# Six row slots instead of eight in a two-layer pooling, attention and expert kernel, with the memory used to keep weight pieces

## What is computed

```python
q = (h @ w_q).reshape(B, S, 8, 2, 128)
s = einsum('bshpc,hpnc->bshpn', q, sub_keys)        # 128 keys in each half
top_s, top_i = top_k(s, 16)                         # then 16 of the 16x16 sums
...
a = einsum('tkd,td->tk', u[ii], hh)                 # 8 heads x 16 experts for each token
w = gg * gelu(a)
return einsum('tk,tkd->td', w, v[ii])
...
x = x + sigmoid(rmsnorm(x) @ ple_wg) * (p @ ple_wp)
```

## Time and profile before

| | |
|---|---|
| Median of 3 runs | 2981.84 us (2978.21 to 2984.22) |
| The profiled execution: time, span | 2986.85 us, 2985.0 us |
| TensorE, VectorE, ScalarE, GpSimd busy | 77%, 74%, 36%, 43% |
| Row gathers, share of the DMA engines | 87.6% |
| Weights and constants, share of the DMA engines | 8.2% |
| Moved in all | 1178.01 MB, mean 395 GB/s |
| Granted TensorE clock, mean | 0.898 |

### The profile page before, as it was taken

The page is one execution under the profiler, slowest core; times in us unless marked ns, Lnnn a source line. Parts: engine busy times, 40 slices in busy tenths (PEclk is TensorE's granted clock), DMA queues, the critical chain, the costliest instruction groups (busy, mean ns, idle before and its releaser), DMA issues.

```text
span 2985.0 us, 23741 instructions
## 1 busy us (share of the span) xinstructions
PE 2284.8 (77%) x6832; PEld 1225.6 (41%) x6832; DVE 2214.6 (74%) x4418; ACT 1074.5 (36%) x3178; POOL 1284.5 (43%) x1028
## 2 busy tenths in 40 slices
PE   3687667977779897888777989789876888665555
PEld 3453224532435454454343545445533444231113
DVE  4585967896687867766979877676596797877774
ACT  1343333333333433643233343355322244333222
POOL 0343453445434444544333444454333344455551
PEclk7889898989989999999988999899998899887777
DMA  4999999999999999999989999999997999999993
GB/s 175 411 364 422 401 420 421 377 420 420 420 380 404 408 421 421 420 420 421 416 331 392 408 408 421 421 408 395 422 420 317 420 381 416 420 419 421 420 420 166
DMA packets 164931, 1178.01 MB, mean 395 GB/s; under 512 B 18496, under 2 KB 19904, under 8 KB 23488
## 3 DMA queue, kind: packets, MB, share of 16 engines
q0 software_dynamic: 147456, 1073.81, 87.6%
q1 hardware_dynamic: 16768, 100.59, 8.2%
q10 hardware_dynamic: 576, 2.10, 0.2%
HBM read 1174.32 MB, written 2.10 MB: 394 GB/s over the span
## 4 chain that ended last, share of the span: by engine, by line
DMA 36%; PE 28%; DVE 24%; issue 5%; ACT 5%; POOL 2%; SPq 0%; ACTq 0%; DVEq 0%; POOLq 0%
DMA slot<-in_uv,idx 35%; PE acc L832 16%; DVE slot L1416 8%; PE M L553 3%; DVE X L1409 3%; PE B L553 2%; POOL slot L530 2%; PE B L625 2%; PE M L625 1%; ACT diag L1028 1%; DVE pos_u L1110 1%; DVE SC L1105 1%; ACT w L1022 1%; DVE best L1108 1%; DVE pos_u L1106 1%
## 5 line engine op out<-in xcount | busy, mean ns | idle before, releaser
L832 PE MATMUL acc<-slot,diag 128*128 128x512 f32 x2908 | 1562.4, 677 | 646.8 <-ACT diag L1028 643.6
L530 POOL DMA_INDIRECT slot<-in_uv,idx x1024 | 1284.3, 1254 | 1644.6 <-PE acc L832 1107.0
L1416 DVE CUSTOM_DVE_ANT_0 slot<-slot,HP 128x1024 f32<-128x1024 f32 x1024 | 1244.9, 1221 | 612.4 <-DMA slot<-in_uv,idx 590.0
L832 PEld LDWEIGHTS acc<-slot,diag 128*128 128x128 f32 x2908 | 574.4, 210 | 1475.9 <-ACT diag L1028 897.7
L1020 ACT ACTIVATE act_a<-a 128x1 f32<-128x1 f32 x1024 | 207.0, 202 | 1705.2 <-DVE a L1416 1692.9
L1409 DVE SCALAR_TENSOR_TENSOR X<-slot,w,X 128x1024 f32<-128x1024 f32 x297 | 380.6, 1281 | 16.5 <-ACT w L1022 16.4
L1022 ACT ACTIVATE w<-act_a,gate 128x1 f32<-128x1 f32 x1024 | 301.6, 295 | 33.2
L1028 ACT ACTIVATE diag<-cst,w 128x128 f32<-128x128 f32 x727 | 291.9, 402 | 23.8
L553 PE MATMUL B<-w,TT 128*128 128x256 f32 x400 | 90.7, 379 | 0.0
L553 PE MATMUL M<-w,TT 128*128 128x256 f32 x400 | 90.6, 379 | 0.0
L625 PE MATMUL M<-TT,w 128*128 128x256 f32 (+1 forms) x448 | 89.7, 356 | 0.0
(11 more groups left out here) (169 smaller groups left out, 1568.1 us busy)
## 6 DMA issues: line engine op xcount, KB each, us to landing
w<-in_wq SPq DMA_DIRECT2D x28, 1024.0 KB
slot<-in_uv,idx POOLq DMA_INDIRECT x1024
w<-in_ple_wg SPq DMA_DIRECT2D x8, 1024.0 KB
w<-in_w_o SPq DMA_DIRECT2D x8, 1024.0 KB
w<-in_w_dq SPq DMA_DIRECT2D x6, 1024.0 KB
w<-in_w_uq_nope SPq DMA_DIRECT2D x8, 768.0 KB
w<-in_ple_wp SPq DMA_DIRECT2D x5, 1024.0 KB
slot<-in_wq SPq DMA_DIRECT2D x4, 1024.0 KB, 10.3
```

Source lines behind the costliest of these rows:

```text
L530: nc.gpsimd.indirect_dma_start(out=slot[s][:], out_offset=None, in_=uv[g // NC], in_offset=bass.IndirectOffsetOnAxis(ap=idx[:, g % HPB, k: ...
L832: last = nc.tensor.matmul(acc[:, half * 512:half * 512 + 512], diag[adds_on_pe(n) % DIAGS][:], slot[s][:, D + half * 512:D + half * 512 + ...
L1416: nc.vector.tensor_tensor_reduce(out=slot[s][:, 0:D], in0=slot[s][:, 0:D], in1=HP[:, g % HPB, :], scale=1.0, scalar=0.0, op0=ALU.mult, op1 ...
```

## The change

SLOTS goes from 8 to 6. A row slot has the size of one weight piece (2048 floats for each of 128 partitions, 1 MB), and the memory of the two slots becomes two places "more" of one piece each, MORE = 2. Pieces 4 and 5 of wq (layer 0) are loaded into them for pair 1 and used again for the group of pairs 2 and 3. After that the two key-value weights w_ukv_k and w_ukv_v are loaded into them for group 4 and used again for group 6. The first of those loads waits for the last use of the wq piece that lay there. Since 128 is no multiple of 6, slots are numbered n % SLOTS over all gathers.

```diff
-SLOTS = 8
+SLOTS = 6
+MORE = 2
...
 KEPT = [("wq", (1, 2)), ("ple_wg", (4, 6, 7))]
+MORE_KEPT = [(("wq", 4), (1, 2)), (("wq", 5), (1, 2)), (("w_ukv_k", 0), (4, 6)), (("w_ukv_v", 0), (4, 6))]
...
+        more = [(j, groups) for j, (kept_piece, groups) in enumerate(MORE_KEPT)
+                if (name, i) == kept_piece and g0 in groups]
         if n < FIRST_PIECES:
             found.append(("slot", FIRST_SLOT + n, 0, None, False))
         elif kept:
             k, groups = kept[0]
             found.append(("KV", i, k, None, g0 != groups[0]))
+        elif more:
+            j, groups = more[0]
+            home = "more", j % MORE
+            if g0 == groups[0] and home in first:
+                had = first[home]
+            else:
+                had = None
+            first[home] = n
+            found.append(home + (j // MORE, had, g0 != groups[0]))
...
+        more = [sb(f"more{i}", [P, PIECE]) for i in range(MORE)]
...
+                    "more": [sem(f"more_loaded{i}") for i in range(MORE)],
...
-                if where == "ring" and had is not None:
+                if where in ("ring", "more") and had is not None:
                     sp.wait_ge(weights_used, had + 1)
...
-                    n, s = g * KSEL + k, k % SLOTS
+                    n, s = g * KSEL + k, (g * KSEL + k) % SLOTS
...
-                s = k % SLOTS
+                s = n % SLOTS
```

More of the change, by code:

```diff
@@ L377, in trunk @@
         slot = [sb(f"slot{i}", [P, 2 * D]) for i in range(SLOTS)]
-        places = {"ring": ring, "slot": slot, "KV": [KV[:, i * PIECE:(i + 1) * PIECE] for i in range(4)]}
+        more = [sb(f"more{i}", [P, PIECE]) for i in range(MORE)]
+        places = {"ring": ring, "slot": slot, "more": more, "KV": [KV[:, i * PIECE:(i + 1) * PIECE] for i in range(4)]}
         diag = [sb(f"diag{i}", [P, P]) for i in range(DIAGS)]
@@ L1015, in gather @@
                 g, k = divmod(n, KSEL)
-                s, half = k % SLOTS, k // (KSEL // 2)
+                s, half = n % SLOTS, k // (KSEL // 2)
                 if k % (KSEL // 2) == 0:
@@ L1405, in add_late @@
                     g, k = divmod(n, KSEL)
-                    s, Xc = k % SLOTS, X[:, g % NC, :]
+                    s, Xc = n % SLOTS, X[:, g % NC, :]
                     dve.wait_ge(weighted, n + 1)
```

## The result

The changed kernel takes 3052.86 us in the median (3052.63 to 3055.03, 4 runs), the kernel before 2980.3 (2978.21 to 2984.22, 4 runs). The ratio is 1.0239, 95% interval 1.0224 to 1.0253: 72.6 us slower. The forecast was +56, with +15 to +105 by its bounds; the way is right, and three terms of the sum turned out to be wrong in size, in both directions.

The account below looks back on a forecast made before the run. The prediction took DMA transfers, mostly row gathers, to bound the kernel, with slots mattering where the consumer is late. Full bursts +50, partial stretches +16 and bytes -10 gave +56 us on 2981.8: 3038 us, range 2997 to 3100.

Parts of the forecast that it names:

- The bound and the cover: Row gathers: DMA-bound; a slot's turn needs 11.8 us, leaving 8.2 us against a late consumer with eight slots, 3.2 with six.
- rival C: Every gather, ordinary stretches too: stage work holds slots longer than 15.0 us, 87 us on top, 3125 us; chance 0.15.
- Rival A: Every stretch: the cover is enough and only bytes count, -10 us, so 2972 us; chance 0.07.
- Rival B: Bursts cost a gather at four or five places only, about +10, cancelled by -10: no change, 2982 us; chance 0.06.
- The bytes, -10: Weight queue: four 1024 KB loads less, 2.49 us each where the DMA is full; -10.0 us, bounds 5 to 10 saved.
- The ten full bursts, 5.0 us each: Ten stretches where eight slots ran out: each pays two gathers once, 5.0 us; +50 in all, bounds +25 to +55.
- The partial stretches, +16: Nine dense stretches at 420 to 422 GB/s where eight slots just held: 1.8 us each, +16, bounds 0 to +45.
- My +0: DMA idle at 1505 and 2246, GpSimd waiting for VectorE's indices: doesn't hang on slots, +0, up to +10.

Follow-up runs that it names:

- the put-in bursts: Unread sums put on VectorE in the last pair, five bursts of 6 us or three of 12: eight slots 2985.09, 2993.62 us; six slots 3063.78, 3080.0 us.

## Why the prediction was right and where it was off

**The bound and the cover.** Right in the quiet pair, in part by luck (see rival C). The queue got shorter (10.10 for 15.08 us), a quiet stretch lost 1% of its rate and the whole last pair 1.5 us, and the put-in bursts cost 0, 2.5, 2.7 and 8.5 us where the cover of 8.2 and 3.2 us says 0, 2.8, 3.8 and 8.8. Rival A, that the cover is enough, is out. Rival B's zero is out as well.

**The bytes, -10.** The term failed: leaving the bytes out is worth 0. For the two key-value loads the step that failed is their place. I named the case (a load inside a stretch that the slots bind is worth nothing) and then decided against it without having looked when SyncE issues them. The row would have said so: 1744.45. For the two wq loads, at 475.82 in a full stretch, the place was right, and why they are worth nothing stays open. What the change wins here, 6 to 11 us over plain slots, is near my number by luck: it isn't the bytes, and the earlier start of the ring's next loads is a possible cause that isn't shown. The price quoted beside this term for a lone 1 MB doesn't hold together (1 MB in 6.15 us is 170 GB/s, not 341); neither number is in the sum.

**The ten full bursts, 5.0 us each.** The step that failed is "as it is full elsewhere nothing gives them back". The ten stretches lost 33 us, 0 to 8.2 each, and with seven slots 9 us where one gather each would be 25. In a long dense stretch VectorE sets the pace for long and the missing rows aren't missed. The clearest is the first, 160 to 198, where VectorE is busy 33.40 of 38 us: it takes 36.3 us with eight, seven and six slots. Around 877 to 917, what VectorE waited for from 858 to 912 before, and for the same gathers (878 to 935) after:

```profile
DVE TT L1366 <- PE T L546: 0.5, 1, 0.5
```

```profile
DVE slot L1431 <- DMA slot<-in_uv,idx: 2.0, 2, 1.6
```

Before, VectorE never waited for rows there. With seven slots it didn't either (865 to 919 has no wait at all), and pair 2 cost 2.5 us in all with seven slots where two of the ten bursts should have made 5. With six slots the rows ran out, twice, and the pair cost 6.9 where the sum has 10. So the first slot is nearly free in such a stretch and the second is less so, which fits a cost of 24 us for one slot and 80 for two. The waits for indices at the ends of the pairs 3 and 5 give nothing back: the dot products were 31.5 us late before the first and 31.3 behind it, 44.6 and 44.3 at the second. My +0 for them was right.

**The partial stretches, +16.** Too small, and it is the largest miss: what the ten didn't lose, some 32 of the 65 us, was lost elsewhere. Pair 6 cost 18.5 us after the change (5 to 7 by my sum) and 8.8 us with seven slots. It holds a stretch that I didn't have in either list, the kernel before from 2475 to 2600 and GpSimd's waits on TensorE in it:

```profile
2475.00:2600.00 125.00, 94.98 (x200) 38.58 (x199) 97.98 (x167) 52.61 (x150) 56.32 (x49) 0.90 1.01 420
```

```profile
POOL slot L530 <- PE acc L832: 56.3, 29, 8.5
```

The DMA moves 420 GB/s, so I passed it by. But the longest wait for a slot is 8.5 us, of eight slots that just held. Roughly the same gathers after the change:

```profile
2537.00:2664.00 127.00, 89.92 (x165) 34.30 (x165) 94.34 (x162) 50.96 (x144) 53.33 (x47) 0.85 0.98 393
```

393 GB/s over 127 us: 27/420 of 127 is 8 us, and the gathers 841 to 889 took 8.4 us longer. The other half of pair 6's loss is the 8.2 us of 2402 to 2475, which I had at 5.0, with a second burst there only as an upper bound. I had looked for partial stretches by the busy share of VectorE and TensorE and given each 1.8 us from one wait of 3.4; the waits for a slot themselves, longest first, in each stretch at full rate, would have found it. Pair 0 cost as much as pair 6: it ended 19.1 us late, 14 to 16 in the other two executions. By the ten bursts it has 10, of which 3.0 came (160 to 198 gave none). With six slots and no kept pieces it was 9 to 11 us late, so some 3 to 10 us of it are the wq pieces loaded early; the rest lies between the stretches that I had listed.

**Rival C** asked for a turn that binds everywhere. With six slots it takes 1.5 us from the last pair (323.4 for 321.9). With five it decides: 363 GB/s, a turn of 14.4 us on average (5 x 1.048 MB at 363), although 11.8 us is what I had worked out as the least. The chain with five slots shows what that left out:

```profile
3113.20 8.62 DMA slot<-in_uv,idx
...
3121.88 1.11 issue
...
3124.12 3.80 PE acc L847 x4
```

I had taken a slot that VectorE frees, 1.2 us of add behind 1.1 of dot product. For a slot that TensorE frees, as most are, 6.1 us pass from the landing to the end of the adds (3121.82 to 3127.92). And the transfer takes 8.62 us though the DMA isn't full, where I had 4.75 from the end of an issue, read where no other gather was under way. Both make the real turn longer; how much each counts wasn't tried. So the cover of 8.2 and 3.2 us rests on a least turn that is too short, and that it priced the put-in bursts so well is not explained by it.

The Trainium skill, Perfetto Trace Analysis, section Optimization Strategy, says that one gap repeated through a stretch, on the engine that should be saturated, can mean too few buffers. That engine is here the DMA. The trace agrees at five slots (a share of 0.96 and 363 GB/s), and at eight and seven there is no such gap (1.01 and 420 GB/s), although GpSimd waits for slots there all the time.

The sum that the runs support: +80 for two slots, -6 to -11 for keeping the pieces elsewhere, 0 for the bytes. That is +69 to +74 for the 72.6 measured, where the forecast had +66 for the slots and -10 for the bytes. The errors of the terms partly cancelled: 17 us too much for the ten stretches, more than that too little for the others, and a -10 that came in another way.

## What to carry to other kernels

Count buffers by the time of one turn: what a slot needs at the least, against slots times the transfer of one. The difference is the cover; a lone delay cost its length less the cover here, to within 1.1 us. Take the turn from every engine that frees slots, and with other transfers under way; else the least turn comes out too short, as it did with five slots. Before giving bytes a price, look at when their load is issued: in a stretch that the buffers bind they can be free, and here even those in a full stretch didn't show. Compare stretches by the same gathers and not by the rate in a window, and don't take a shorter wait for time won: look at when it ends. And flattening the work that holds the buffers (12 us here with eight slots, 33 with six) is to be tried before buffers are traded for anything.

## What was not expected of the hardware

Four transfers of 1 MB left out changed nothing measurable on DMA engines that are busy 96% of the span (87.6% and 8.2% in the earlier trace rows). And from six to five slots the rate of 1 MB gathers in a quiet stretch fell from 416 to 363 GB/s at once, while from eight to seven it did not move from 420. With five slots a transfer in the chain still took 8.62 us, with the DMA's share at 0.96; in the earlier trace rows a gather landed within 4.75 us of its issue's end when no other was under way.
